# Two squared-ReLU MLPs on one Trainium2 core: weight sums and early low parts move from GpSimd to VectorE, and the squares read PSUM

## The chip, the cores and the metric

The program runs on one core of one Trainium2 chip. The engines are TensorE (PE; its weight loads are PEld), VectorE (DVE), ScalarE (ACT), GpSimd (POOL) and SyncE (SP), which issues most DMAs. Each works through its own list of instructions in order and waits on semaphores for the others. The metric is the device time of the program in microseconds (us): 2716.86 us is the median of 3 runs before the change (2715.68 to 2720.47).

## What is computed

Two layers of a diffusion backbone with 1024 latent tokens, 256 context tokens and 1024 channels. Layer 0 mixes tokens with a Fourier mixer, layer 1 with windowed attention; each is followed by the same MLP, which is what the change touches:

```python
D_MODEL, SEQ, CTX_LEN, DEPTH, D_FF = 1024, 1024, 256, 2, 4096

def _sq_relu_mlp(h, w1, w2):
    return jnp.square(jax.nn.relu(h @ w1)) @ w2

# per layer i, after the mixer
h_lat = h_lat + g2 * _sq_relu_mlp(_modulate(_rms_norm(h_lat, norm2_g[i]), sh2, sc2), mlp_w1[i], mlp_w2[i])
if not last:   # layer 0 alone
    h_ctx = h_ctx + cg2 * _sq_relu_mlp(_modulate(_rms_norm(h_ctx, norm2_g[i]), csh2, csc2), mlp_w1[i], mlp_w2[i])
```

## The kernel before

**Numbers in two parts.** Every fp32 operand of a matmul is split into a rounded high part and a low part (full minus high), and a product is three matmuls: high by high, high by low, low by high (`mm3`, and lines 1293 to 1295). High parts are copies on ScalarE. Low parts are subtractions (`lo_part`, line 58), on VectorE for activations (`l_al`, `l_acl`, `nl`) and on GpSimd for both weights (`l_w1l`, `l_w2l`).

**Pairs.** `mlp` is called once per layer. It goes over the 4096 hidden rows in 16 pairs of 128-row chunks. The latent tokens are two blocks of 512, and layer 0 has the 256 context tokens as a third block. A pair has two products. In the **first product** PE makes `z` for each block and chunk (lines 51 to 53, 24 matmuls each): B11, B12, B22, B21 by block and chunk, and in layer 0 also C0 and C1 for the context. ScalarE applies ReLU from PSUM (`relu`, line 935) into a slot, VectorE squares the slot in place (`square`, line 1123), ScalarE makes the high part (`high`, line 946), VectorE the low part (`low`). The **second product** is done in the Strassen-Winograd manner with 7 block products in place of 8 (`ROWS`: M5, M3, M2, M1, M6, M7, M4). It needs four differences of the hidden blocks, T1 to T4 (`diff`, line 1137, VectorE), and four sums of the second weights' blocks, S1 to S4 (`summed`, line 858, GpSimd). M5 is S1 by T1, M3 is S4 by B22, M2 is A12 by B21, M1 is A11 by B11, M6 is S2 by T2, M7 is S3 by T3, M4 is A22 by T4. Each product is 4 groups of 3 matmuls, one group for each of the four PSUM banks `l_yy_ps`. In layer 0 four context groups (`ctx`, bank `l_yc_ps`) stand among them.

**Reading the groups.** VectorE adds groups 0 to 2 of every product into `ht` with the gate as scale (`acc`, line 1144: PSUM by gate plus `ht`). Group 3 goes through ScalarE (`side_read`, line 953, PSUM into one of two `side` buffers) and GpSimd (`add`, line 880). A PSUM bank is written again only when its last reader is done (`freed`), so M3's group 0 waits for the addition of M5's group 0, and so on.

**What sets the order.** Each engine's list is written out by hand in `mlp`: `hidden` and `outputs` on VectorE and PE, `pair` and `outputs` on ScalarE, `weights` and `outputs` on GpSimd, loads on SP. VectorE's `outputs` puts the difference T4 behind M5's three additions, the low part of B21 (which M2 waits for) behind M3's first, and the low part of T4 behind M2's first. ScalarE's `pair` copies the weights' high parts (`high2`, line 927) between the ReLUs: S1 and A11 behind B11's, A12 and S4 behind B12's. GpSimd's `weights` makes sums and low parts in turn: S1, its low part, S2, A11's low part, S3, A12's low part, S4, S4's low part. Then come the two low parts of the next pair's first weights (`low1`, 1024 wide), then the low parts of the later second weights among the four-bank additions.

**Loads.** SP's list for pair p is `load1(p, 0)`, `load1(p, 1)`, `load2(p)`. A chunk of the first weights is loaded when GpSimd has made the low part of the chunk before it. The second weights of a pair are loaded when all `l_w2l` of the pair before are made. ScalarE's `high1` (line 920) copies a chunk's high part: in pair p, chunk 0 of pair p+1 before B22's ReLU, chunk 1 at the start of `outputs`, ahead of the high part of B21 and the first `side_read`.

## Time and profile before

| | |
|---|---|
| median of 3 runs | 2716.86 us |
| the profiled execution | 2721.47 us, its span 2719.8 us |
| mean granted TensorE clock, share of full speed | 0.955 |
| PE busy | 2406.9 us (88%), 11716 matmuls |
| DVE busy | 1739.2 us (64%) |
| POOL busy | 1205.6 us (44%) |
| ACT busy | 1121.2 us (41%) |
| GpSimd: low parts of second weights (line 58) | 240 of 1372 ns mean |
| GpSimd: sums of second weights (line 858) | 128 of 1375 ns mean |
| GpSimd: low parts of first weights (line 58) | 64 of 2397 ns mean |
| VectorE: squares 512 wide (line 1123) | 128 of 1266 ns mean |

PE is the engine that is busy nearly throughout, so what counts in the two MLPs is where PE stands idle. The share of busy time says little about the others; the timeline does, where it shows which of them ended PE's wait. Layer 0's MLP takes the span from 402.42 to 1298.98 us, layer 1's from 1939.38 us to the end.

### The profile page before, as it was taken

Reading aid. Unit: us, or ns where it says so; the run is one execution under the profiler, and the core shown is the slowest. Engines: PE = TensorE matmul, PEld = TensorE weight load, DVE = VectorE, ACT = ScalarE, POOL = GpSimd, SP = SyncE. Lnnn points to the kernel's source line nnn. Section 1 sums busy time; section 2 is a strip of 40 time slices with the busy share of each in tenths; the row PEclk is TensorE's granted clock in tenths of the full one; section 3 lists DMA queues with packets and bytes.
Section 4 is the critical chain, followed back from the end, with each engine's and each line's share of the span. In section 5 each row is a group of like instructions: output and inputs, shape, how many; then the busy total and the mean of one; then the engine's idle time right before and its main releaser. Section 6 shows DMA issues by size and latency. Waiting matters only on the chain. (4 is left out here: it accounts for less than half of the span.)

```text
span 2719.8 us, 36933 instructions
## 1 busy us (share of the span) xinstructions
PE 2406.9 (88%) x11716; PEld 1941.5 (71%) x11716; DVE 1739.2 (64%) x2705; ACT 1121.2 (41%) x2036; POOL 1205.6 (44%) x927
## 2 busy tenths in 40 slices
PE   4988968999999999999497888879879999898988
PEld 2667847888888788878286666658567777777777
DVE  4557776566656665566676788862556565757565
ACT  4442143333333333333532788860533333333333
POOL 0000034556555555555200455540256666666664
PEclk9998989999999999999799899989889999999999
DMA  6437511010101111010221211112111110111112
GB/s 229 144 109 278 201 66 36 32 39 31 54 31 36 34 49 36 31 39 16 98 72 51 55 28 28 24 46 78 39 39 54 39 54 31 44 49 39 54 39 78
DMA packets 89164, 171.66 MB, mean 63 GB/s; under 512 B 38145, under 2 KB 48897, under 8 KB 82689
## 3 DMA queue, kind: packets, MB, share of 16 engines
q1 hardware_dynamic: 82416, 137.73, 15.1%
q0 software_dynamic: 3456, 25.17, 2.5%
q10 hardware_dynamic: 3216, 7.86, 0.8%
q8 instruction: 35, 0.57, 0.1%
q14 instruction: 41, 0.33, 0.0%
HBM read 158.16 MB, written 12.58 MB: 63 GB/s over the span
## 5 line engine op out<-in xcount | busy, mean ns | idle before, releaser
L1144 DVE SCALAR_TENSOR_TENSOR ht<-l_yy_ps,mod,ht 128x512 f32<-128x512 f32 x672 | 470.0, 745 | 48.5 <-PE l_yy_ps L1295 48.1
L51 PE MATMUL l_z_ps<-nh,l_w1h 128*128 128x512 f32 (+1 forms) x1280 | 475.3, 371 | 10.1 <-DVE nl L58 4.7
L52 PE MATMUL l_z_ps<-nl,l_w1h 128*128 128x512 f32 (+1 forms) x1280 | 473.4, 370 | 0.0
L53 PE MATMUL l_z_ps<-nh,l_w1l 128*128 128x512 f32 (+1 forms) x1280 | 472.8, 369 | 0.0
L1293 PE MATMUL l_yy_ps<-l_ah,l_w2h 128*128 128x512 f32 x896 | 370.4, 413 | 101.3 <-DVE ht L1144 60.6
L58 POOL TENSOR_TENSOR l_w2l<-l_w2f,l_w2h 128x512 fp32r<-128x512 f32 x240 | 328.5, 1372 | 293.7 <-ACT l_w2h L927 288.6
L880 POOL TENSOR_TENSOR ht<-ht,l_side 128x512 f32<-128x512 f32 x224 | 312.2, 1394 | 183.4 <-ACT l_side L953 179.1
L1123 DVE TENSOR_TENSOR l_slot<-l_slot 128x512 f32<-128x512 f32 x128 | 161.9, 1266 | 360.9 <-ACT l_slot L935 360.7
L1294 PE MATMUL l_yy_ps<-l_al,l_w2h 128*128 128x512 f32 x896 | 361.4, 403 | 0.0
L1295 PE MATMUL l_yy_ps<-l_ah,l_w2l 128*128 128x512 f32 x896 | 360.7, 403 | 0.0
L953 ACT ACTIVATE l_side<-l_yy_ps,mod 128x512 f32<-128x512 f32 x224 | 153.4, 685 | 363.8 <-PE l_yy_ps L1295 363.8
L1293 PEld LDWEIGHTS l_yy_ps<-l_ah,l_w2h 128*128 128x128 f32 x896 | 175.8, 196 | 164.2 <-issue 67.7
L51 PEld LDWEIGHTS l_z_ps<-nh,l_w1h 128*128 128x128 f32 x1280 | 243.0, 190 | 54.9 <-DVE nl L58 7.7
L52 PEld LDWEIGHTS l_z_ps<-nl,l_w1h 128*128 128x128 f32 x1280 | 243.1, 190 | 40.4 <-issue 0.5
L53 PEld LDWEIGHTS l_z_ps<-nh,l_w1l 128*128 128x128 f32 x1280 | 242.9, 190 | 40.5
L946 ACT ACTIVATE l_ah<-l_slot 128x512 fp32r<-128x512 f32 x224 | 140.1, 630 | 286.9 <-DVE l_slot L1123 106.4
L58 POOL TENSOR_TENSOR l_w1l<-l_w1f,l_w1h 128x1024 fp32r<-128x1024 f32 x64 | 153.4, 2397 | 236.6 <-ACT l_w1h L920 236.6
L58 DVE TENSOR_TENSOR l_al<-l_slot,l_ah 128x512 fp32r<-128x512 f32 x224 | 174.3, 802 | 52.5 <-ACT l_ah L946 52.5
L1295 PEld LDWEIGHTS l_yy_ps<-l_ah,l_w2l 128*128 128x128 f32 x896 | 175.0, 195 | 39.2
L1294 PEld LDWEIGHTS l_yy_ps<-l_al,l_w2h 128*128 128x128 f32 x896 | 176.9, 197 | 31.2
L927 ACT ACTIVATE l_w2h<-l_w2f 128x512 fp32r<-128x512 f32 x240 | 144.4, 621 | 106.5 <-POOL l_w2f L858 95.6
L858 POOL TENSOR_TENSOR l_w2f<-l_w2f 128x512 f32<-128x512 f32 x128 | 176.0, 1375 | 13.7 <-DMA l_w2f<-w 6.2
(223 smaller groups left out, 4492.9 us busy)
## 6 DMA issues: line engine op xcount, KB each, us to landing
l_w1f<-w SPq DMA_DIRECT2D x64, 512.0 KB, 3.4
l_w2f<-w SPq DMA_DIRECT2D x64, 512.0 KB, 4.2
maw<-ada SPq DMA_DIRECT2D x24, 1024.0 KB, 5.2
aw<-ada POOLq DMA_DIRECT2D x24, 1024.0 KB, 5.1
qb<-queries SPq DMA_DIRECT2D x64, 128.0 KB, 2.7
fw<-fnet_w SPq DMA_DIRECT2D x8, 512.0 KB, 4.5
fx<-x SPq DMA_DIRECT2D x8, 512.0 KB, 5.3
park<-ht SPq DMA_DIRECT2D x1, 4096.0 KB, 12.0
```

Source lines behind the costliest of these rows:

```text
L51: pe.matmul(out, lh, rh, start=first, stop=False)
L52: pe.matmul(out, lh, rl, start=False, stop=False)
L53: return pe.matmul(out, ll, rh, start=False, stop=last)
L58: return eng.tensor_tensor(lo, full, f32(hi), ALU.subtract)
L858: pool.tensor_tensor(w2f[:, PLACE[name]], w2f[:, PLACE[a]], w2f[:, PLACE[b]], op).then_inc(s_sum, 1)
L880: pool.tensor_tensor(h, h, side[(i - 1) % 2][:], ALU.add).then_inc(s_add, 1)
L953: act.activation(side[(i - 1) % 2][:], y_ps[SIDE][:], ACT.Copy, scale=mod[:, layer, G2, m, 0:1]).then_inc(s_ya, 1)
L1123: dve.tensor_tensor(s, s, s, ALU.mult).then_inc(s_sqr, 1)
L1144: dve.scalar_tensor_tensor(out=h, in0=y_ps[m][:], scalar=mod[:, layer, G2, c, 0:1], in1=h, op0=ALU.mult, op1=ALU.add).then_inc(s_acc, 1)
L1293: pe.matmul(y_ps[m][:], wh, a_h, start=first, stop=False, skip_group_check=not first)
L1294: pe.matmul(y_ps[m][:], wh, a_l, start=False, stop=False, skip_group_check=not first)
L1295: pe.matmul(y_ps[m][:], wl, a_h, start=False, stop=True, skip_group_check=not first).then_inc(s_y, 1)
```

## The change

It has six parts, all inside `mlp`:

1. `square` becomes one scalar_tensor_tensor, `max(z, 0) * relu`: its first input is the PSUM bank, its second the slot with ReLU's result. A `z` bank is therefore free for PE when the square is done (`s_sqr`), not when ReLU is (`s_rel`).
2. S1 to S4 and the low parts of S1, A11, A12 and S4 go from GpSimd to VectorE. `weights` stands at the head of VectorE's `hidden`; S4's low part stands behind B11's.
3. GpSimd keeps the low parts of S2, S3, A22 (and A21), of the first weights, and the additions. It has no work in the first product. `low1(p+1, 0)` stands behind the addition of M3, `low1(p+1, 1)` ahead of that of M6.
4. ScalarE copies the high parts of S1, A11 and A12 ahead of B11's ReLU and that of S4 behind B11's high part. `high1(p+1, 1)` moves from the head of `outputs` to the place behind M1's `side_read` (in layer 0 behind A21's high part), ahead of M6's. In layer 1, A22's high part goes ahead of M1's `side_read`.
5. In VectorE's `hidden`, B22's low part stands ahead of the difference T3.
6. One semaphore for the second weights' low parts becomes two (`s_w2e` for the early four, `s_w2l` for the late ones), and `load2` waits for the late ones.

The order of PE's products does not change.

```diff
-    W_ORDER = ["S1", "A11", "A12", "S4", "S2", "S3", "A22"] + (["A21"] if C else [])
+    W_EARLY = ["S1", "A11", "A12", "S4"]
+    W_LATE = ["S2", "S3", "A22"] + (["A21"] if C else [])
+    W_ORDER = W_EARLY + W_LATE
...
                 def load2(p, rows):
-                    sp.wait_ge(s_w2l, p * NW + PRE)
+                    sp.wait_ge(s_w2l, p * NL + PRE)
...
             def _(pool):
                 def outputs(p, more):
+                    add(p, "M5")
+                    low2(p, "S2")
+                    add(p, "M3")
+                    if more:
+                        low1(p + 1, 0)
+                    low2(p, "S3")
+                    add(p, "M2")
+                    if C:
+                        add(p, "M1")
+                    for name in W_LATE[2:]:
+                        low2(p, name)
+                    if not C:
+                        add(p, "M1")
                     if more:
                         low1(p + 1, 1)
-                    low2(p, "S2")
-                    add(p, "M5")
-                    low2(p, "S3")
-                    for prod in ("M3", "M2", "M1"):
-                        add(p, prod)
-                    for name in W_ORDER[6:]:
-                        low2(p, name)
                     for prod in ("M6", "M7", "M4"):
                         add(p, prod)
...
             def _(act):
                 def outputs(p, order, more):
-                    if more:
-                        act.wait_ge(s_z, p * U1 + (PRE + U1))
-                        high1(p + 1, 1)
                     high(p, "B21", order)
                     side_read(p, "M5")
...
                     side_read(p, "M2")
+                    if not C:
+                        high2(p, "A22")
                     side_read(p, "M1")
                     if C:
                         act.wait_ge(s_y, p * NG + (PRE + Y_AT["ctx", 1] + 1))
-                    for name in W_ORDER[6:]:
+                        high2(p, "A22")
+                        high2(p, "A21")
+                    if more:
+                        high1(p + 1, 1)
+
+                def pair(p, more=True):
+                    for name in ("S1", "A11", "A12"):
                         high2(p, name)
                     relu(p, "B11", Z_LOOP)
                     high(p, "B11", Z_LOOP)
-                    for name in ("S1", "A11"):
-                        high2(p, name)
+                    high2(p, "S4")
                     relu(p, "B12", Z_LOOP)
                     high(p, "T1", Z_LOOP)
-                    for name in ("A12", "S4"):
-                        high2(p, name)
...
             def _(dve):
                 def square(p, name, order):
                     s = source(name)
+                    pos = order.index(name)
+                    n = TB[TOK[name][0]][1]
                     dve.wait_ge(s_rel, z_at(p, name, order))
-                    dve.tensor_tensor(s, s, s, ALU.mult).then_inc(s_sqr, 1)
+                    dve.scalar_tensor_tensor(out=s, in0=z_ps[pos % NZ][:, 0:n], scalar=0.0, in1=s, op0=ALU.max, op1=ALU.mult).then_inc(s_sqr, 1)
...
+                def weights(p):
+                    dve.wait_ge(s_w2, p * 32 + 32)
+                    summed(p, "S1", "A21", ALU.add, "A22")
+                    low2(p, "S1")
+                    replaces(p, "S2", "S1")
+                    summed(p, "S2", "S1", ALU.subtract, "A11")
+                    low2(p, "A11")
+                    replaces(p, "S3", "A11")
+                    summed(p, "S3", "A11", ALU.subtract, "A21")
+                    low2(p, "A12")
+                    replaces(p, "S4", "A12")
+                    summed(p, "S4", "A12", ALU.subtract, "S2")
+
                 def hidden(p):
+                    weights(p)
                     square(p, "B11", Z_LOOP)
                     low(p, "B11", HI_LOOP)
+                    low2(p, "S4")
                     square(p, "B12", Z_LOOP)
...
             def _(pe):
-                        pe.wait_ge(s_rel, p * U1 + (PRE + pos - NZ + 1))
+                        pe.wait_ge(s_sqr, p * U1 + (PRE + pos - NZ + 1))
```

How the lists change is best seen in the first pair of layer 1, which stands outside the loop; the loop has the same order but for one `high1`. The names are those of the tiles (`l_w2f` the second weights, `l_w2h` and `l_w2l` their parts, `l_w1l` the first weights' low part, `l_ah` and `l_al` the hidden blocks' parts); "x3" stands for three in a row. Line numbers of the changed program are its own: 871 is `add`, 945 `side_read`, 919 `high2`, 938 `high`, 912 `high1`, 1142 `summed`, 1105 `square`.

GpSimd, from the last sum to the end of the pair, before:

```order
L858 TENSOR_TENSOR l_w2f<-l_w2f 128x512
L58 TENSOR_TENSOR l_w2l<-l_w2f,l_w2h 128x512
L58 TENSOR_TENSOR l_w1l<-l_w1f,l_w1h 128x1024 x2
L58 TENSOR_TENSOR l_w2l<-l_w2f,l_w2h 128x512
L880 TENSOR_TENSOR ht<-ht,l_side 128x512
L58 TENSOR_TENSOR l_w2l<-l_w2f,l_w2h 128x512
L880 TENSOR_TENSOR ht<-ht,l_side 128x512 x3
L58 TENSOR_TENSOR l_w2l<-l_w2f,l_w2h 128x512
L880 TENSOR_TENSOR ht<-ht,l_side 128x512 x3
```

and all of the pair after, on the same engine:

```order
L871 TENSOR_TENSOR ht<-ht,l_side 128x512
L58 TENSOR_TENSOR l_w2l<-l_w2f,l_w2h 128x512
L871 TENSOR_TENSOR ht<-ht,l_side 128x512
L58 TENSOR_TENSOR l_w1l<-l_w1f,l_w1h 128x1024
L58 TENSOR_TENSOR l_w2l<-l_w2f,l_w2h 128x512
L871 TENSOR_TENSOR ht<-ht,l_side 128x512
L58 TENSOR_TENSOR l_w2l<-l_w2f,l_w2h 128x512
L871 TENSOR_TENSOR ht<-ht,l_side 128x512
L58 TENSOR_TENSOR l_w1l<-l_w1f,l_w1h 128x1024
L871 TENSOR_TENSOR ht<-ht,l_side 128x512 x3
```

The sums and four low parts are gone, the addition of M5 comes first, and the two 1024-wide low parts stand apart, among the additions.

ScalarE from the high parts of B22, T2 and T3 to the end of the pair, before:

```order
L946 ACTIVATE l_ah<-l_slot 128x512 x3
L920 ACTIVATE l_w1h<-l_w1f 128x1024 x2
L946 ACTIVATE l_ah<-l_slot 128x512
L953 ACTIVATE l_side<-l_yy_ps,mod 128x512
L927 ACTIVATE l_w2h<-l_w2f 128x512
L946 ACTIVATE l_ah<-l_slot 128x512
L953 ACTIVATE l_side<-l_yy_ps,mod 128x512
L927 ACTIVATE l_w2h<-l_w2f 128x512
L953 ACTIVATE l_side<-l_yy_ps,mod 128x512 x2
L927 ACTIVATE l_w2h<-l_w2f 128x512
L953 ACTIVATE l_side<-l_yy_ps,mod 128x512 x3
```

and after:

```order
L912 ACTIVATE l_w1h<-l_w1f 128x1024
L938 ACTIVATE l_ah<-l_slot 128x512
L945 ACTIVATE l_side<-l_yy_ps,mod 128x512
L919 ACTIVATE l_w2h<-l_w2f 128x512
L938 ACTIVATE l_ah<-l_slot 128x512
L945 ACTIVATE l_side<-l_yy_ps,mod 128x512
L919 ACTIVATE l_w2h<-l_w2f 128x512
L945 ACTIVATE l_side<-l_yy_ps,mod 128x512
L919 ACTIVATE l_w2h<-l_w2f 128x512
L945 ACTIVATE l_side<-l_yy_ps,mod 128x512
L912 ACTIVATE l_w1h<-l_w1f 128x1024
L945 ACTIVATE l_side<-l_yy_ps,mod 128x512 x3
```

The second copy of the first weights now stands behind four side reads and ahead of the last three.

VectorE from the first square to the additions of M5, before:

```order
L1123 TENSOR_TENSOR l_slot<-l_slot 128x512
L58 TENSOR_TENSOR l_al<-l_slot,l_ah 128x512
L1123 TENSOR_TENSOR l_slot<-l_slot 128x512 x2
L1137 TENSOR_TENSOR l_slot<-l_slot 128x512
L58 TENSOR_TENSOR l_al<-l_slot,l_ah 128x512
L1123 TENSOR_TENSOR l_slot<-l_slot 128x512
L1137 TENSOR_TENSOR l_slot<-l_slot 128x512 x2
L58 TENSOR_TENSOR l_al<-l_slot,l_ah 128x512 x3
L1144 SCALAR_TENSOR_TENSOR ht<-l_yy_ps,mod,ht 128x512 x3
```

and after, up to the two squares:

```order
L1142 TENSOR_TENSOR l_w2f<-l_w2f 128x512
L58 TENSOR_TENSOR l_w2l<-l_w2f,l_w2h 128x512
L1142 TENSOR_TENSOR l_w2f<-l_w2f 128x512
L58 TENSOR_TENSOR l_w2l<-l_w2f,l_w2h 128x512
L1142 TENSOR_TENSOR l_w2f<-l_w2f 128x512
L58 TENSOR_TENSOR l_w2l<-l_w2f,l_w2h 128x512
L1142 TENSOR_TENSOR l_w2f<-l_w2f 128x512
L1105 SCALAR_TENSOR_TENSOR l_slot<-l_z_ps,l_slot 128x512
L58 TENSOR_TENSOR l_al<-l_slot,l_ah 128x512
L58 TENSOR_TENSOR l_w2l<-l_w2f,l_w2h 128x512
L1105 SCALAR_TENSOR_TENSOR l_slot<-l_z_ps,l_slot 128x512 x2
```

Seven instructions on the second weights stand ahead of the first square, and an eighth behind the first low part.

## Rows read from the trace of the kernel before

**Rows 1.** Stretches: bounds, length, then PE, PEld, DVE, ACT, POOL busy, clock, DMA.

```profile
470.62:1243.02 772.40, 742.87 (x3867) 631.20 (x3866) 488.36 (x672) 262.75 (x448) 430.94 (x295) 1.00 0.11 37
2010.96:2661.38 650.42, 600.13 (x2521) 487.52 (x2520) 404.06 (x505) 235.75 (x378) 411.29 (x280) 0.96 0.13 45
1939.38:2010.96 71.58, 53.15 (x183) 39.15 (x182) 53.26 (x66) 37.00 (x56) 30.89 (x20) 0.82 0.14 45
```

**Rows 2.** The same columns: first product of layer 0, then of layer 1.

```profile
691.32:718.88 27.56, 27.56 (x146) 23.77 (x145) 12.34 (x14) 8.87 (x16) 13.91 (x10) 1.00 0.05 18
2010.96:2032.71 21.75, 21.75 (x97) 18.02 (x96) 6.30 (x7) 6.78 (x11) 13.04 (x10) 1.00 0.06 23
```

**Rows 3.** Waits, 14 pairs of layer 0: who for whom, us, times, longest.

```profile
PE l_yy_ps L1293 <- DVE l_al L58: 19.1, 14, 1.4
PE l_yy_ps L1293 <- DVE ht L1144: 10.4, 14, 0.7
```

**Rows 4.** Waits, 14 pairs of layer 1.

```profile
PE l_yy_ps L1293 <- DVE ht L1144: 49.2, 14, 3.5
```

**Rows 5.** Timeline of PE, layer 1: start, us, instruction, [idle before it, who ended it].

```profile
2039.10 0.49 PE L1293 MATMUL l_yy_ps<-l_ah,l_w2h 128*128 128x512 f32 x1 [3.50 <-DVE ht L1144]
2043.21 0.50 PE L1293 MATMUL l_yy_ps<-l_ah,l_w2h 128*128 128x512 f32 x1 [1.12 <-DVE l_al L58]
...
2687.03 0.50 PE L1293 MATMUL l_yy_ps<-l_ah,l_w2h 128*128 128x512 f32 x1 [1.01 <-DVE ht L1144]
2690.73 0.47 PE L1293 MATMUL l_yy_ps<-l_ah,l_w2h 128*128 128x512 f32 x1 [0.68 <-DVE l_al L58]
```

**Rows 6.** Timeline of ACT, the same pair of layer 1.

```profile
2022.04 0.60 ACT L935 ACTIVATE l_slot<-l_z_ps 128x512 f32<-128x512 f32 x1 [2.33 <-PE l_z_ps L53]
...
2029.58 0.63 ACT L927 ACTIVATE l_w2h<-l_w2f 128x512 fp32r<-128x512 f32 x1 [2.77 <-POOL l_w2f L858]
...
2031.06 0.58 ACT L935 ACTIVATE l_slot<-l_z_ps 128x512 f32<-128x512 f32 x1
```

**Rows 7.** Timeline of DVE, the same pair.

```profile
2031.67 2.81 DVE L1123 TENSOR_TENSOR l_slot<-l_slot 128x512 f32<-128x512 f32 x1 [4.66 <-ACT l_slot L935]
...
2038.13 2.06 DVE L1144 SCALAR_TENSOR_TENSOR ht<-l_yy_ps,mod,ht 128x512 f32<-128x512 f32 x3
...
2042.05 1.11 DVE L58 TENSOR_TENSOR l_al<-l_slot,l_ah 128x512 fp32r<-128x512 f32 x1
```

**Rows 8.** Timeline of POOL, the same pair.

```profile
2031.54 2.40 POOL L58 TENSOR_TENSOR l_w1l<-l_w1f,l_w1h 128x1024 fp32r<-128x1024 f32 x1
...
2040.86 1.75 POOL L58 TENSOR_TENSOR l_w2l<-l_w2f,l_w2h 128x512 fp32r<-128x512 f32 x1
```

**Rows 9.** Views of single lines: count, shortest/median/longest ns, first and last start.

```profile
L1123 DVE TENSOR_TENSOR l_slot<-l_slot x128: 677/694/2811, 411.3 to 2685.6; 128x512 f32<-128x512 f32 x128
...
L1144 DVE SCALAR_TENSOR_TENSOR ht<-l_yy_ps,mod,ht x672: 731/744/753, 438.2 to 2708.6; 128x512 f32<-128x512 f32 x168
...
L858 POOL TENSOR_TENSOR l_w2f<-l_w2f x128: 1262/1289/1727, 408.2 to 2678.6; 128x512 f32<-128x512 f32 x128
```

**Rows 10.** Timeline of PE, first pair of layer 0, then of layer 1.

```profile
447.08 0.79 PE L1293 MATMUL l_yy_ps<-l_ah,l_w2h 128*128 128x512 f32 x1 [5.71 <-ACT l_side L953]
...
1981.63 0.77 PE L1293 MATMUL l_yy_ps<-l_ah,l_w2h 128*128 128x512 f32 x1 [7.66 <-DVE l_al L58]
1993.15 0.79 PE L1293 MATMUL l_yy_ps<-l_ah,l_w2h 128*128 128x512 f32 x1 [4.42 <-ACT l_side L953]
```

**Rows 11.** Timeline of ACT, first pair of layer 1.

```profile
1976.19 0.63 ACT L927 ACTIVATE l_w2h<-l_w2f 128x512 fp32r<-128x512 f32 x1 [5.76 <-POOL l_w2f L858]
...
1990.95 1.06 ACT L920 ACTIVATE l_w1h<-l_w1f 128x1024 fp32r<-128x1024 f32 x1 [5.92 <-DMA l_w1f<-w]
```

**Rows 12.** DMA issues: instruction, count, KB each, median us to landing.

```profile
l_w1f<-w SPq DMA_DIRECT2D x64, 512.0 KB, 3.4
l_w2f<-w SPq DMA_DIRECT2D x64, 512.0 KB, 4.2
```

More of the change, by code:

```diff
@@ L1027, in _ @@
                 norm(1)
-                for name in ("S1", "A11"):
+                for name in ("S1", "A11", "A12"):
                     high2(0, name)
@@ L1032, in _ @@
                 high(0, "B11", Z_FIRST)
-                for name in ("A12", "S4"):
-                    high2(0, name)
+                high2(0, "S4")
                 if C:
@@ L1049, in _ @@
                 outputs(0, Z_FIRST, True)
+                for prod in ("M6", "M7", "M4"):
+                    side_read(0, prod)
                 with act.Fori(1, PAIRS - 1) as p:
                     pair(p)
-                pair(PAIRS - 1, False)
+                    for prod in ("M6", "M7", "M4"):
+                        side_read(p, prod)
                 last = PAIRS - 1
+                pair(last, False)
                 def out_half(i):
@@ L1165, in hidden @@
                     diff(p, "T2", "B22", "T1", Z_LOOP, HI_LOOP)
+                    low(p, "B22", HI_LOOP)
                     diff(p, "T3", "B22", "B12", Z_LOOP, HI_LOOP)
-                    for name in ("B22", "T2", "T3"):
+                    for name in ("T2", "T3"):
                         low(p, name, HI_LOOP)
@@ L1202, in _ @@
                 norm(1)
+                weights(0)
                 dve.wait_ge(s_nl, 2 * KC)
@@ L1275, in group @@
                             pe.wait_ge(s_al, p * NH + (PRE + horder.index("C1") + 1))
-                            pe.wait_ge(s_w2l, p * NW + (PRE + W_ORDER.index("A12" if m < 2 else "A21") + 1))
+                            for c in range(2):
+                                split2(pe, p, "A%d%d" % (1 + m // 2, c + 1))
                         for j in range(2):
```

67 lines of the change are left out of this document (22 added, 45 removed).

## The prediction, made before the changed kernel ran

> **What bounds the kernel now.** I read the stretches first, then PE's waits, then the timelines of the engines that ended them. The reader should see a pair as a sum: matmuls without a gap, plus what is lost. In the first product nothing is lost: 96 matmuls of 512 columns take 21.75 us in layer 1, 0.2266 us each, and layer 0's 27.56 us hold the same 96 and 5.81 us of context matmuls, PE busy throughout [rows 2]. A pair of layer 1 has 180 matmuls, 40.8 us; the 14 loop pairs take 650.42 / 14 = 46.46 us each, so 5.66 us are lost. A pair of layer 0 would take 27.56 + 84 x 0.2266 + 5.81 = 52.4 us; it takes 772.40 / 14 = 55.17, so 2.77 us are lost [rows 1]. All of it lies in the second product. Over 28 pairs that is 118 us, nearly the ceiling of what any edit to the loops can give.
>
> The waits say where. In layer 1, PE stands 3.50 us in front of M3 (an addition of M5 is late) and 1.12 us in front of M2 (the low part of B21 is late) [rows 4, 5]. In layer 0 it is 10.4 / 14 = 0.74 and 19.1 / 14 = 1.36 us, the same two places [rows 3]. The rest, 1.04 us and 0.67 us a pair, follows the waits: the first matmul takes 0.49 where others take less [rows 5], and in layer 1 the granted clock is 0.96 of full where layer 0's stays at 1.00 [rows 1], so some matmuls run at 1.2 GHz in place of 2.4. I count 0.35 us for each wait that stays and stays short (0.67 / 2).
>
> Why M5's additions are late is seen on the other engines. GpSimd's last sum, S4, comes so late that ScalarE idles 2.77 us for it, up to 2029.58, and B22's ReLU stands behind it in ScalarE's list and starts at 2031.06 [rows 6]. B12's ReLU starts 11.08 us after its first product does, 0.2 us behind the 10.88 us of its two z [rows 2, 6]; B22's could so have started at 2010.96 + 16.3 + 0.2 = 2027.5. It is 3.6 us late, which is the M3 wait. Then the square takes 2.81 us in place of a median 0.69, and ends 0.54 us after a 2.40 us GpSimd low part that had begun just before it [rows 7, 8, 9].
>
> **The change part by part.** *Squares from PSUM.* They take the form of the additions (PSUM and SBUF in, SBUF out): 672 of those took 731 to 753 ns, whatever GpSimd did, while the squares had a median of 694 and went up to 2811 [rows 9]. I take 744, so 0.05 us more on each square that nobody disturbs. One per pair lies on the path (the last before M5's additions): 32 x 0.05 = 1.6 us. The bank is held 0.75 us longer; PE writes it again three or four z later, at least 10 us on, so this is free. The Trainium skill speaks against this part: "VectorE: DVE Perf Modes", section on the TRN2 errata, gives a fixed 120 cycles for a source in PSUM and 58 in SBUF; by its 62 cycles at 0.96 GHz, an estimate of 0.065 us, the part would cost 2.1 us.
>
> *Sums and early low parts on VectorE.* Eight instructions of 0.69 us where GpSimd needed 1.29 [rows 9], and one handover to ScalarE for S1 (0.63 and two short gaps): 5.6 us ahead of B11's square, 0.7 us behind its low part. They start when the last additions are done and the second weights are there. GpSimd's low part of A22 ends about 15 us into the second product by the sum of its new list (six operations of 1.3 us and one of 2.4 from 4.2 us on, with their waits); the load takes 4.2 us each for two issues [rows 12], so it lands about when the product ends. S4 is then ready some 7 us into the first product; before, ScalarE had it 18.6 us in (2029.58). T1 is the first thing that needs these squares, behind B12's ReLU at 11.1 us: 4 us of slack hide the block. Without that cover it would cost what it exceeds, microsecond for microsecond.
>
> *ScalarE.* No copy of a weight stands in front of a late ReLU, so B22's starts at about 16.5 us. M3's wait goes. What is late next is M2's operand. I count from M5's first matmul in layer 1: B21's ReLU ends at 0.8, its square at 1.6, M5's three additions (2.06 [rows 7]) at 3.65, T4 (0.69) at 4.35, M3's first addition at 5.1, and the low part of B21 at 5.8 undisturbed or 6.2 with the 1.11 us that it took beside GpSimd [rows 7, 8]. M2 is due after 24 matmuls, at 5.44. GpSimd's addition of M5 starts at 4.2 in the new list (M5's group 3 ends at 2.9, then the high part of B21 and the side read), so it runs beside this low part: I take 6.2, a wait of 0.7, with bounds of 0.3 and 1.1 (the last pair, where GpSimd had no first weights, shows 0.68; the loop 1.12 [rows 5]). M5's additions precede M3's groups by 0.4 us or more. New loss in layer 1: 0.7 + 0.35 = 1.05, gain 4.6 a pair.
>
> In layer 0 the last block is C1, half as wide, and square, high and low part come before the additions: with half-wide steps bounded by nothing and the full 0.6 to 0.7 each, the additions begin between 0.8 and 2.9; I take 2.0. The same chain ends at 6.5, a wait of 1.05. Loss 1.4, gain 1.4 a pair.
>
> *The first weights' low parts and the load.* `low1` of chunk 0 now ends about 11 us into the second product, chunk 1 lands 3.4 us later [rows 12], at 14.5, and ScalarE copies it until 15.6, ahead of M6's side read, which is due at about 15. PE wants that bank for M7's last group at about 16.6. So it costs nothing in layer 1 with 0.3 us to spare, and in layer 0, whose context groups put M6 3 us later, with more.
>
> *First pairs.* The copy of chunk 1 stood at the head of ScalarE's second product and waited 5.92 us for its DMA in layer 1; the side read of M5 behind it held PE 4.42 us, in layer 0 5.71 [rows 10, 11]. Both go, since that copy now has four side reads before it. PE's 7.66 us before M5 in layer 1 end when T1 is ready, which waited on S4 (ScalarE idle 5.76 us [rows 11]); between nothing and 7.66 comes back, I take 3. For half-rate matmuls (the stretch has a mean clock of 0.82 [rows 1]) I add 2 in each layer: 7.7 + 9.4 = 17, bounds 10 and 24. *Last pair* of layer 1: M3's 1.01 us [rows 5].
>
> **Sum.** 14 x 4.6 + 14 x 1.4 + 17 + 1 = 102 us. The profiled execution took 2721.5, 4.6 us above the median of 2716.9; on the median that gives 2615 us. By the bounds: M2's waits at 0.3 and 0.5 and first pairs at 24 give 2716.9 - 122 = 2595; M2's waits at 1.1 and 1.9 and first pairs at 10 give 2716.9 - 78 = 2639.
>
> **The rivals.** *VectorE falls behind in the second product* (2628 to 2655). If GpSimd's operations catch both low parts in full, B21's and T4's, each loses up to 1.3 us, and the additions of M2 that stand behind T4's low part hold M1 as well. M2's and M1's waits then come to about 2.4 us a pair in both layers and only M3's waits are gained: 14 x (3.50 + 0.74) + 17 + 1 = 77, so 2640. For it: the low part of B21 is caught in the old loop in both layers. Against: later additions have 2.72 us of matmuls for three of 0.70, so 0.6 us per product is made good. The Trainium skill has this as a rule: "SBUF — State Buffer", section "Who interferes with whom", says that a VectorE instruction with two SBUF inputs and a GpSimd instruction that reads SBUF lock each other out for a whole instruction. The trace agrees (2.81 us for 0.69, ending 0.54 us behind GpSimd [rows 7, 8]).
>
> *GpSimd goes on into the next pair.* Its last additions run up to 3 us into the first product and catch VectorE's first sums: 2.6 us more at most, inside the 4 us of slack, no change of time.
>
> *The load stands in front of the side reads* (slower). If the copy of chunk 1 is late, M6's side read is, and PE stops in M7: every us beyond 0.3 (layer 1) or 3 (layer 0) is paid in each pair. To end above 2717 it must cost 102 us, so be late by some 5.4 us in both layers: 14 x (5.1 + 2.4) = 105, 2720 us. ScalarE did wait 5.92 us for this DMA in the first pair [rows 11], but from the end of its previous copy, and with a load time of 3.4 us [rows 12]. A lateness of 1 us costs 10 us.
>
> *The change doesn't do what it says* (M3's wait stays, about 2700): B22's ReLU would have to be late for another reason than S4. 3.6 us late against a wait of 3.50 leaves little.
>
> **How the numbers follow.** The forecast, 2615, has 0.70 (its own range 2595 to 2630). VectorE behind has 0.15, a partial gain between 2650 and 2705 (a late load, or M3's wait staying) has 0.06, less than 2595 (M2's wait gone too) 0.03, nothing at all 0.02, slower 0.04. The range 2595 to 2648 leaves out the last four and the tail of the second: 2 in 10 at most. About 0.2% (5 us) is what a measurement of this kernel can tell from no change: faster 0.94, same 0.02, slower 0.04.
>
> **What would show it.** M3's waits for an addition gone in both layers; one wait of 0.3 to 1.9 us a pair left, in front of M2, ended by the low part of B21; a pair at 41.9 us in layer 1 and 53.8 in layer 0; clock 1.00 in layer 1's loop; squares at 0.74 us without outliers; GpSimd idle in the first product; ScalarE waiting for the first weights' DMA by a few us per pair without PE waiting for the side read. Wrong would be: PE waiting in the first product, or in front of M7 for a side read (the load), or in front of M5 for the low part of T1 (VectorE's new block in the way).

## The result, and the profile after

The changed kernel takes 2609.28 us, the median of four runs from 2607.88 to 2612.35, where the kernel before took 2716.70. The ratio is 0.9604 with a 95% interval from 0.9587 to 0.962: 107 us gained, where 102 were forecast, and the time lies inside the range. The profiled execution after took 2608.24 us with a span of 2606.6; against the profiled one of before that is 113 us, about 6 more than the medians show, since that one had been 4.6 us above its median and this one is 1.0 below.

The stretches after, with the columns of [rows 1]: the 14 loop pairs of layer 0, those of layer 1, the first pair of layer 1, and one first product of layer 1.

```profile
460.40:1208.02 747.62, 741.70 (x3866) 631.24 (x3865) 490.11 (x784) 270.29 (x448) 275.88 (x183) 1.00 0.11 39
1962.39:2549.70 587.31, 579.19 (x2522) 469.74 (x2520) 441.28 (x617) 238.99 (x378) 259.73 (x169) 1.00 0.15 50
1900.36:1962.39 62.03, 50.69 (x182) 37.93 (x181) 54.34 (x74) 37.00 (x56) 18.21 (x12) 0.84 0.15 52
1962.39:1984.15 21.76, 21.76 (x97) 18.02 (x96) 14.02 (x20) 8.79 (x14) 2.83 (x2) 1.00 0.06 23
```

Against [rows 1], layer 0's loop gives back 772.40 - 747.62 = 24.8 us (53.40 us a pair), layer 1's 650.42 - 587.31 = 63.1 (41.95 a pair), and layer 1's first pair 71.58 - 62.03 = 9.6. The first pair of layer 0 goes from 68.20 to 58.45, another 9.8, and the two last pairs give 2.0. These make 109 us; the other 4 of the span lie in code that the change does not touch: from layer 0's last addition to layer 1's first product it took 641.4 us before and 637.8 after, and from 635.8 to 644.6 over all kernels run here. The first product is as long as in [rows 2], 21.76 us, but VectorE works 14.02 us in it where it worked 6.30, and GpSimd 2.83 where it worked 13.04. Layer 1's loop has its clock at 1.00, where [rows 1] had 0.96.

The waits of PE after, first of layer 0's 14 pairs, then of layer 1's (who for whom, us, times, longest). The waits for an addition of [rows 3, 4] are gone. Those for a low part fall from 19.1 to 5.9 us in layer 0; in layer 1, where the view of before has one of 1.1 us in the 14 pairs (the third line), each pair now has one.

```profile
PE l_yy_ps L1306 <- DVE l_al L58: 5.9, 14, 0.4
```

```profile
PE l_yy_ps L1306 <- DVE l_al L58: 8.1, 14, 0.6
```

```profile
PE l_yy_ps L1293 <- DVE l_al L58: 1.1, 1, 1.1
```

The timelines of one second product of layer 1, which starts at 1984.15, answer [rows 5 to 8]. PE, then DVE, POOL and ACT:

```profile
1990.33 0.50 PE L1306 MATMUL l_yy_ps<-l_ah,l_w2h 128*128 128x512 f32 x1 [0.58 <-DVE l_al L58]
```

```profile
1984.98 0.69 DVE L1105 SCALAR_TENSOR_TENSOR l_slot<-l_z_ps,l_slot 128x512 f32<-128x512 f32 x1 [1.36 <-ACT l_slot L927]
1985.59 2.06 DVE L1126 SCALAR_TENSOR_TENSOR ht<-l_yy_ps,mod,ht 128x512 f32<-128x512 f32 x3
...
1988.83 1.45 DVE L58 TENSOR_TENSOR l_al<-l_slot,l_ah 128x512 fp32r<-128x512 f32 x1
```

```profile
1988.44 1.29 POOL L871 TENSOR_TENSOR ht<-ht,l_side 128x512 f32<-128x512 f32 x1 [23.07 <-ACT l_side L945]
```

```profile
1984.35 0.60 ACT L927 ACTIVATE l_slot<-l_z_ps 128x512 f32<-128x512 f32 x1 [1.46 <-PE l_z_ps L53]
...
1999.38 1.06 ACT L912 ACTIVATE l_w1h<-l_w1f 128x1024 fp32r<-128x1024 f32 x1 [2.27 <-DMA l_w1f<-w]
```

The last ReLU now waits for nothing but its own z, the last square takes 0.69 us, M5's additions start 1.44 us into the product, and M3 does not wait. What is left is the low part of B21: 1.45 us beside GpSimd's addition of M5, which had begun 0.39 us before it, and so PE stands 0.58 us in front of M2. ScalarE does wait 2.27 us for the first weights' DMA, and PE not for the side read behind it.

The squares and the additions after, as [rows 9] has them (shortest, median, longest ns):

```profile
L1105 DVE SCALAR_TENSOR_TENSOR l_slot<-l_z_ps,l_slot x128: 681/691/692, 414.3 to 2572.3; 128x512 f32<-128x512 f32 x128
L1126 DVE SCALAR_TENSOR_TENSOR ht<-l_yy_ps,mod,ht x672: 733/743/753, 435.5 to 2595.3; 128x512 f32<-128x512 f32 x168
```

The first pairs after, on PE, against [rows 10]: the waits of 5.71 and 4.42 us for a side read are gone, short waits for the same two places as in the loop have come (0.82 and 1.60, and 0.61), and 5.01 of the 7.66 us before M5 have stayed.

```profile
436.27 0.50 PE L1306 MATMUL l_yy_ps<-l_ah,l_w2h 128*128 128x512 f32 x1 [0.82 <-DVE ht L1126]
440.89 0.47 PE L1306 MATMUL l_yy_ps<-l_ah,l_w2h 128*128 128x512 f32 x1 [1.60 <-DVE l_al L58]
...
1940.06 0.77 PE L1306 MATMUL l_yy_ps<-l_ah,l_w2h 128*128 128x512 f32 x1 [5.01 <-DVE l_al L58]
1948.55 0.47 PE L1306 MATMUL l_yy_ps<-l_ah,l_w2h 128*128 128x512 f32 x1 [0.61 <-DVE l_al L58]
```

### The profile page after: what moved, and what is told of

The parts are those of the page before. It is cut to its first block and busy times, and to the rows that moved or that the text cites. A ratio compares the mean times of both kernels' runs of the same rounds, so it can differ in the third digit from the quotient of the medians.

```text
span 2606.6 us, 37012 instructions
## 1 busy us (share of the span) xinstructions
PE 2374.1 (91%) x11716; PEld 1917.2 (74%) x11716; DVE 1787.0 (69%) x2961; ACT 1131.9 (43%) x2036; POOL 854.7 (33%) x671
## 5 line engine op out<-in xcount | busy, mean ns | idle before, releaser
L871 POOL TENSOR_TENSOR ht<-ht,l_side 128x512 f32<-128x512 f32 x224 | 294.8, 1316 | 940.0 <-ACT l_side L945 933.5
L1306 PE MATMUL l_yy_ps<-l_ah,l_w2h 128*128 128x512 f32 x896 | 358.2, 400 | 23.4 <-DVE l_al L58 22.6
L1307 PE MATMUL l_yy_ps<-l_al,l_w2h 128*128 128x512 f32 x896 | 351.4, 392 | 0.0
L1308 PE MATMUL l_yy_ps<-l_ah,l_w2l 128*128 128x512 f32 x896 | 350.3, 391 | 0.0
L1105 DVE SCALAR_TENSOR_TENSOR l_slot<-l_z_ps,l_slot 128x512 f32<-128x512 f32 x128 | 88.1, 689 | 210.6 <-ACT l_slot L927 210.5
L58 DVE TENSOR_TENSOR l_al<-l_slot,l_ah 128x512 fp32r<-128x512 f32 x224 | 186.5, 834 | 47.6 <-ACT l_ah L938 44.7
L1307 PEld LDWEIGHTS l_yy_ps<-l_al,l_w2h 128*128 128x128 f32 x896 | 169.1, 189 | 27.6
L927 ACT ACTIVATE l_slot<-l_z_ps 128x512 f32<-128x512 f32 x128 | 76.2, 597 | 259.6 <-PE l_z_ps L53 259.6
L58 POOL TENSOR_TENSOR l_w1l<-l_w1f,l_w1h 128x1024 fp32r<-128x1024 f32 x64 | 167.4, 2615 | 28.4 <-ACT l_w1h L912 28.4
L1722 POOL TENSOR_TENSOR sc<-sc,den 128x640 f32<-128x640 f32 x128 | 156.4, 1253 | 18.6 <-DVE den L1816 18.6
```

What stands on the lines that cost most here:

```text
L58: return eng.tensor_tensor(lo, full, f32(hi), ALU.subtract)
L871: pool.tensor_tensor(h, h, side[(i - 1) % 2][:], ALU.add).then_inc(s_add, 1)
L1306: pe.matmul(y_ps[m][:], wh, a_h, start=first, stop=False, skip_group_check=not first)
L1307: pe.matmul(y_ps[m][:], wh, a_l, start=False, stop=False, skip_group_check=not first)
L1308: pe.matmul(y_ps[m][:], wl, a_h, start=False, stop=True, skip_group_check=not first).then_inc(s_y, 1)
L1722: pool.tensor_tensor(sc[:, i, h, 0:KEYS], sc[:, i, h, 0:KEYS], den[:, i, h:h + 1].to_broadcast([P, KEYS]), ALU.mult).then_inc(s_p, 1)
```

## Experiments on what carried the gain

Six kernels do one part alone, undo one, or load one. All times are medians of four runs with the kernel before on the same chip (2716 to 2718 us).

**The squares undone** in the changed kernel: VectorE squares the block in SBUF, and PE's wait for the bank is again one on the ReLU.

```diff
-dve.scalar_tensor_tensor(out=s, in0=z_ps[pos % NZ][:, 0:n], scalar=0.0, in1=s, op0=ALU.max, op1=ALU.mult)
+dve.tensor_tensor(s, s, s, ALU.mult)
```

> The changed kernel, with one part undone: the squares again multiply the slot by itself in SBUF, and PE's next z waits for the ReLU. The theory (order: the gain comes from taking B22's ReLU off the chain of weight sums, and the copy of the first weights off the head of ScalarE's second product) expects no difference: GpSimd is idle throughout the first product in the changed kernel, so a square in SBUF meets nobody. 2609 us, within 4. The rival (squares: reading PSUM keeps the squares out of GpSimd's way, and that is half of the gain) expects the 2.1 us of the old B22 square back in each of 28 pairs: 2609 + 59 = 2668 us.

It took 2609.06 us (ratio 0.9606, 0.959 to 0.9622), as the whole change. Its squares, by the view of their line:

```profile
L1105 DVE TENSOR_TENSOR l_slot<-l_slot x128: 684/692/694, 411.5 to 2567.2; 128x512 f32<-128x512 f32 x128
```

They take the same 0.69 us without one outlier: with nothing of GpSimd left in the first product, there is nothing to escape from.

**The squares alone**, the same edit the other way, put into the kernel before.

> The kernel before, with one part done: squares read PSUM, the rest as it was. The theory expects little: B22's ReLU is still 3.6 us late, and the instruction behind the square, the difference T2, has two SBUF inputs and meets the same 2.40 us GpSimd operation, so it ends about 0.7 us sooner and no more. 28 x 0.7 = 20: 2697 us, PE's wait in front of M3 in layer 1 from 3.5 to about 2.8 us. The rival (squares) expects the whole 2.1 us: 28 x 2.1 = 59, 2658 us, that wait at 1.4 us.

It took 2688.87 us (0.9901, 0.9884 to 0.9918): 28 us gained alone, somewhat more than the 20 expected. PE in one pair of layer 1, and the squares of this kernel:

```profile
2112.73 0.49 PE L1295 MATMUL l_yy_ps<-l_ah,l_w2h 128*128 128x512 f32 x1 [1.55 <-DVE ht L1146]
2117.47 0.50 PE L1295 MATMUL l_yy_ps<-l_ah,l_w2h 128*128 128x512 f32 x1 [1.73 <-DVE l_al L58]
```

```profile
L1125 DVE SCALAR_TENSOR_TENSOR l_slot<-l_z_ps,l_slot x128: 675/691/693, 410.9 to 2652.0; 128x512 f32<-128x512 f32 x128
```

No square is held any more, though GpSimd still works through the first product. M3's wait fell from 3.50 [rows 5] to 1.55, near the 1.4 of the rival, while 1.66 to 1.88 us are lost in front of M2. As the theory had it, the difference T2 now meets the GpSimd operation in the square's place and is held, so this part of the chain gained 0.7 us only; but B22's ReLU also starts 18.9 us into the first product, where it started at 20.1 [rows 2, 6], since S4 came earlier too. In layer 0 M3's wait is gone, and M2 waits 1.37 us as before.

**ScalarE's copies alone** in the new order, in the kernel before.

```diff
+act.wait_ge(s_y, p * NG + PRE)
+for name in ("S1", "A11", "A12"):
+    high2(p, name)
...
-for name in ("S1", "A11"):
-    high2(p, name)
+high2(p, "S4")
...
-for name in ("A12", "S4"):
-    high2(p, name)
```

> The kernel before with ScalarE's copies alone in the new order (S1 and the high parts ahead of the last block's ReLU, S4 behind its high part); squares, sums, low parts and first weights stay where they are. Theory (the order of ScalarE's copies carries most of layer 1): the waits before the second product's M3 go down to about 1 us a pair, 14 x 3.6 + 14 x 0.9 = 63 us, so about 2654. Rival (the order needs the sums on VectorE or the early first weights with it): about 2700, with M3's wait of about 3 us still there.

It took 2671.35 us (0.9826, 0.9808 to 0.9844): 45 us, between the two expectations. PE in one pair of layer 1, and the squares of this kernel:

```profile
2028.56 0.49 PE L1293 MATMUL l_yy_ps<-l_ah,l_w2h 128*128 128x512 f32 x1 [1.06 <-DVE ht L1144]
2032.67 0.50 PE L1293 MATMUL l_yy_ps<-l_ah,l_w2h 128*128 128x512 f32 x1 [1.11 <-DVE l_al L58]
```

```profile
L1123 DVE TENSOR_TENSOR l_slot<-l_slot x128: 679/1174/2506, 411.2 to 2638.7; 128x512 f32<-128x512 f32 x128
```

M3's wait falls to 1.06 us here and 1.11 in the later pairs, as the theory had it, and about 1 us is still lost in front of M2 (0.95 to 1.20 us of standing). So a pair of layer 1 is 2.65 us shorter, 2.4 of them from M3's wait, and not 3.6 us; in layer 0 it is 0.80, not 0.9. That is where the forecast of 2654 failed. What stays of M3's wait: a square that meets GpSimd's long low part still takes up to 2.51 us, and the ReLU and the low parts behind it come late with it.

**First weights back** at their old places, in the changed kernel: GpSimd's low parts for the next pair and ScalarE's second copy for it at the head of the second product (the lines at their new places go).

```diff
 def outputs(p, more):            # GpSimd
+    if more:
+        low1(p + 1, 0)
+        low1(p + 1, 1)
...
 def outputs(p, order, more):     # ScalarE
+    if more:
+        act.wait_ge(s_z, p * U1 + (PRE + U1))
+        high1(p + 1, 1)
```

> The changed kernel, with one part undone: both low parts of the next pair's first weights again at the head of GpSimd's list for the second product, and the copy of chunk 1 again at the head of ScalarE's. Sums stay on VectorE. The theory expects the first pairs' waits back (5.7 and 4.4 us, with some half-rate matmuls 12 in all) and about 0.5 us a pair more in front of M2, because a 2.40 us GpSimd operation runs from about 2 to 4.3 us and pushes T4, the addition of M5 and B21's low part: 2609 + 12 + 13 = 2634 us. If the place of the first weights costs nothing, 2609; if it carries half of the gain, 2660.

It took 2641.37 us (0.9722, 0.9706 to 0.9738), 7 us above the 2634 expected: undone in the finished kernel, the new places are worth 32 us. By the starts of PE's matmuls 15 of them are the first pairs (66.5 and 69.3 us, after 58.5 and 62.0), 13 are layer 0, where M2 waits 1.37 us in place of 0.42, and 4 are layer 1.

**Sums and early low parts on GpSimd** as before, with everything else of the change in place.

```diff
+def weights(p):                  # GpSimd, ahead of outputs(p)
+    pool.wait_ge(s_w2, p * 32 + 32)
+    summed(p, "S1", "A21", ALU.add, "A22")
+    early2(p, "S1")
...
 def pair(p, more=True):          # ScalarE
+    act.wait_ge(s_y, p * NG + PRE)
     for name in ("S1", "A11", "A12"):
...
 def hidden(p):                   # VectorE
-    weights(p)
     square(p, "B11", Z_LOOP)
     low(p, "B11", HI_LOOP)
-    low2(p, "S4")
```

> The changed kernel, with the sums and the four early low parts done by GpSimd again, at the head of its list for a pair, but in the new order: ScalarE still copies S1, A11 and A12 ahead of B11's ReLU, and the first weights stay among the additions. (ScalarE waits for the pair before to be done ahead of its first copy, which it reaches later anyhow.) The theory (order) expects nearly the same time: nine operations of 1.29 us and one copy from about 2.3 us on give S4 at about 13 us of the first product, 2 us after B12's ReLU is due and 3.5 us before B22's; T1 is still in time. Loops unchanged, first pairs 3 to 5 us longer: 2614 us. The rival (engine: it needs VectorE's speed) expects the wait in front of M3 in layer 1 back, 14 x 3.6 = 50, and layer 0's, 14 x 0.9 = 13: 2670 us.

It took 2613.75 us (0.9619, 0.9603 to 0.9635), where 2614 was expected. The pairs of both layers are as long as after the change; what was lost, 4.5 us, lies in the first pairs. So with the rest of the change in place VectorE's speed on these operations, 0.69 us where GpSimd needs 1.29 [rows 9], hardly counts. This kernel squares from PSUM; with squares in SBUF as well it was not run.

**Six more operations on VectorE** per pair of layer 1, behind the last sum: 512 columns each, into a scratch tile that nobody reads.

```diff
+for i in range(EXTRA):
+    dve.wait_ge(s_dum, p * EXTRA + i + PRE)
+    dve.tensor_tensor(scratch[:], w2f[:, PLACE["A22"]], w2f[:, PLACE["S2"]], ALU.subtract).then_inc(s_dum, 1)
```

> The changed kernel with work added: in layer 1, six subtractions of 512 columns into a scratch tile on VectorE behind the sum S4, ahead of B11's square, in every pair (0.72 us each with their waits, 4.3 us). The theory says that the block of weight work is hidden because nothing needs B11's square before B12's ReLU is through: S4 was ready 7 us into the first product and B12's ReLU starts at 11.1, so 4 us more fit: 2609 us, within 4. The rival (VectorE's work in the first product is paid) expects 14 x 4.3 = 60: 2669 us.

It took 2613.51 us (0.9617, 0.9601 to 0.9633). In DVE's timeline the six stand just ahead of the first square:

```profile
2058.41 4.31 DVE L1167 TENSOR_TENSOR l_scratch<-l_w2f 128x512 f32<-128x512 f32 x6
2062.65 0.68 DVE L1109 SCALAR_TENSOR_TENSOR l_slot<-l_z_ps,l_slot 128x512 f32<-128x512 f32 x1
```

Some 60 us more of VectorE's work in 14 pairs left these pairs at 41.9 us; only the first pair, which has no cover, is longer, by 4. The slack of 4 us that the prediction gave the block is there, and there is more: B12's ReLU, which was to be the first to suffer, starts 13.0 us into the first product in place of 11.1, and nothing is lost by it.

The parts therefore do not add up as one would like. Squares alone are worth 28 us, copies alone 45; yet with GpSimd's sums, early low parts and first weights out of the first product, the squares are worth nothing. The squares' edit and the emptying of GpSimd's list remove the same cause, a GpSimd operation beside a square, so where the list is emptied the squares have nothing left to gain.

## Experiments on the wait that was left

**Addition behind the low part** (the add-after-low kernel): GpSimd's addition of M5 also waits until the low part of B21 is done.

```diff
+pool.wait_ge(s_al, p * NH + (PRE + HI_LOOP.index("B21") + 1))
 add(p, "M5")
```

> The changed kernel, with one wait added on GpSimd: its addition of M5 waits for the low part of B21, so that the two no longer run at the same time. The theory (the wait that is left in front of M2 is this collision: the low part took 1.45 us in layer 1 and 1.12 in layer 0 where 0.69 is its undisturbed time) expects M2's wait gone in layer 1 (0.58 us idle, 0.74 with the slower restart) and nearly gone in layer 0 (0.42). But all of GpSimd's list stands 1.1 us later, the load of the next first weights with it, ScalarE's copy of chunk 1 then ends after M7's last group wants its bank, and in layer 1 about 1 us a pair is lost there: 2609 - 14 x 0.4 + 14 x 0.4 = 2609, within 8, with a wait of PE for a side read that was not there. The rival (VectorE is simply late with M5's additions) expects M2's wait to stay as it is, and 2609.

It took 2611.75 us (0.9612, 0.9596 to 0.9628), the same time as the change, and as the theory had it: M2's wait gone, a side read in its place. The rival, which gave the same time, had M2's wait staying. DVE's low part of B21, then PE and ACT in the same product:

```profile
2067.65 0.68 DVE L58 TENSOR_TENSOR l_al<-l_slot,l_ah 128x512 fp32r<-128x512 f32 x1
```

```profile
2072.40 0.50 PE L1307 MATMUL l_yy_ps<-l_ah,l_w2h 128*128 128x512 f32 x1 [0.28 <-DVE ht L1127]
2080.27 0.50 PE L1307 MATMUL l_yy_ps<-l_ah,l_w2h 128*128 128x512 f32 x1 [0.73 <-ACT l_side L946]
```

```profile
2078.58 1.06 ACT L913 ACTIVATE l_w1h<-l_w1f 128x1024 fp32r<-128x1024 f32 x1 [3.01 <-DMA l_w1f<-w]
2079.55 0.67 ACT L946 ACTIVATE l_side<-l_yy_ps,mod 128x512 f32<-128x512 f32 x1
```

The low part falls from 1.45 to 0.68 us and M2's wait is gone, so GpSimd beside it was the cause. In layer 0 a pair gains 0.4 us. In layer 1 PE, now earlier, waits 0.28 us for an addition and then meets the side read behind ScalarE's copy, which waits for the DMA (GpSimd's list, held by the new wait, lets the load begin later too): the late load, one of the prediction's rivals, is the next limit, worth 0.73 us here.

**The copy behind M6's side read** as well.

```diff
 def outputs(p, order, more):
...
+        side_read(p, "M6")
         high1(p + 1, 1)
...
-for prod in ("M6", "M7", "M4"):
+for prod in ("M7", "M4"):
```

> The add-after-low kernel with ScalarE's high part for the next pair put behind M6's side read. Theory (the wait on the side read in layer 1 comes from ScalarE being held by the DMA for that high part): the wait on the side read goes, layer 1's second product takes 19.8 us and layer 0's 25.4, so about 2597. Rival (the side read is late for its own reasons, or the low part of M7 takes the wait over): no gain, 2609 to 2612.

It took 2596.19 us (0.9557, 0.9541 to 0.9573). No pair waits for a side read, layer 1's second product takes 19.75 us and layer 0's 25.44, all as expected.

**Low part first** (the low-part-first kernel): in the changed kernel VectorE takes the low part of B21 right behind M5's additions, and T4 with its low part later, the latter ahead of M2's third addition. ScalarE's copy of T4 goes later with it.

```diff
 for m in range(3):
     acc(p, "M5", m)
-diff(p, "T4", "B21", "T2", zorder, horder)
-acc(p, "M3", 0)
 low(p, "B21", horder)
-acc(p, "M3", 1)
-acc(p, "M3", 2)
+for m in range(3):
+    acc(p, "M3", m)
+diff(p, "T4", "B21", "T2", zorder, horder)
 acc(p, "M2", 0)
-low(p, "T4", horder)
 acc(p, "M2", 1)
+low(p, "T4", horder)
 acc(p, "M2", 2)
...
 high2(p, "S2")                   # ScalarE
-high(p, "T4", order)
 side_read(p, "M3")
 high2(p, "S3")
+high(p, "T4", order)
```

> The changed kernel, reordered on two engines: VectorE makes the low part of B21 directly behind M5's three additions, then M3's three additions, then T4, and T4's low part behind M2's second addition; ScalarE copies T4 behind M3's side read. The low part then ends at 4.3 us of the second product, before GpSimd's addition of M5 begins and before M2 is due at 5.5. The theory expects M2's wait gone in both layers, 14 x (0.74 + 0.58) = 18 us, less what the load of the first weights takes back in layer 1 (M6's side read stands behind a copy that ends 15.5 us in, PE wants the bank at 15.8: up to 0.5 us a pair, 7): 2591 to 2598 us. The rival (VectorE has too much to do there, the wait moves to M3's or M2's additions) expects 2605 to 2612, with PE waiting for an addition instead.

It took 2649.82 us (0.9748, 0.9732 to 0.9764), 40 us slower than the change, against both theories. One product of layer 1 on PE, DVE and POOL:

```profile
2007.64 0.50 PE L1305 MATMUL l_yy_ps<-l_ah,l_w2h 128*128 128x512 f32 x1 [2.24 <-DVE ht L1126]
```

```profile
1999.09 0.69 DVE L58 TENSOR_TENSOR l_al<-l_slot,l_ah 128x512 fp32r<-128x512 f32 x1
...
2004.13 2.80 DVE L58 TENSOR_TENSOR l_al<-l_slot,l_ah 128x512 fp32r<-128x512 f32 x1
2006.85 2.71 DVE L1126 SCALAR_TENSOR_TENSOR ht<-l_yy_ps,mod,ht 128x512 f32<-128x512 f32 x4
```

```profile
2004.01 2.37 POOL L58 TENSOR_TENSOR l_w1l<-l_w1f,l_w1h 128x1024 fp32r<-128x1024 f32 x1
```

M2's wait is gone, as meant. But T4's low part was issued 0.12 us after GpSimd's long low part and ended 0.55 us after that one's end; M2's third addition stands behind it, and PE stands 2.24 us, some 10 us into the product, for the bank which that addition empties (the third group of M1 wants it). Layer 1 pays twice, as two successive pairs show (bounds, length, busy times, then the granted clock):

```profile
2105.94:2151.09 45.15, 42.91 (x182) 34.82 (x180) 32.71 (x45) 17.13 (x27) 18.27 (x12) 0.96 0.14 46
2062.37:2105.94 43.57, 41.33 (x181) 33.63 (x180) 32.60 (x45) 17.14 (x27) 18.26 (x12) 1.00 0.14 48
```

Every second pair is 1.6 us longer at a clock of 0.96: behind that wait six to eight of its matmuls start 0.43 us apart where the others do 0.23, at a granted clock of 0.51 (2140.9 to 2143.3), that is 1.2 GHz in place of 2.4. The same kernel with **ScalarE's copy later** (the edit above) kept the wait:

> As e5_low_first, and ScalarE's copy of chunk 1 moved behind M6's side read, so that no side read of M6 waits for a load. The theory expects no wait of PE left in either loop: 2609 - 18 = 2591 us, a pair of layer 1 at 41.1 to 41.2 us, of layer 0 at 52.8. If the load did no harm in e5, the two are equal; if the copy now holds M7's side read, PE waits in front of M4's last group and the time is above e5's.

It took 2650.28 us (0.9753, 0.9737 to 0.9769). So the place of ScalarE's copy has no part in it.

**T4's low part behind M2's third addition**, on top of that, with GpSimd's list left alone:

```diff
 acc(p, "M2", 1)
-low(p, "T4", horder)
 acc(p, "M2", 2)
+low(p, "T4", horder)
```

> The low-part-first kernel with T4's low part behind M2's third addition, and GpSimd's list left as it was (its long low part for the next pair ahead of that of S3). Theory (whichever VectorE operation on two SBUF tiles is issued while GpSimd's long operation runs waits for its end): M2's additions are no longer held, so the wait of 2.24 us before M2 goes, but T4's low part is held until about 11.4 us into layer 1's second product where it was needed by 10.3, so PE waits about 1.1 us before M1 in each of 14 pairs and the time is 2601 to 2617. Rival (the place of T4's low part alone decides, GpSimd's order does not matter): no wait, 2586 to 2590.

It took 2602.83 us (0.9583, 0.9567 to 0.9599). DVE, POOL and PE in one product of layer 1, which starts at 2016.63:

```profile
2025.92 2.17 DVE L58 TENSOR_TENSOR l_al<-l_slot,l_ah 128x512 fp32r<-128x512 f32 x1
```

```profile
2025.14 2.40 POOL L58 TENSOR_TENSOR l_w1l<-l_w1f,l_w1h 128x1024 fp32r<-128x1024 f32 x1
```

```profile
2028.98 0.49 PE L1306 MATMUL l_yy_ps<-l_ah,l_w2h 128*128 128x512 f32 x1 [1.05 <-DVE ht L1127]
```

The low part, issued 0.78 us into GpSimd's operation, is held again, and PE waits 1.05 us where 1.1 were expected. It does so in front of M6 and not of M1, and it waits for the bank of the addition behind the low part, not for the low part itself.

**GpSimd's low part of S3 ahead of its long one** in addition:

```diff
 add(p, "M3")
+low2(p, "S3")
 if more:
     low1(p + 1, 0)
-low2(p, "S3")
```

> The low-part-first kernel with T4's low part behind M2's third addition, and GpSimd's low part of S3 ahead of its low part for the next pair. Theory (the slower time came from T4's low part issued just behind GpSimd's long operation and from nothing else): the wait of 2.24 us before M2's last matmuls goes to about 0.15, so 2591 to 2597. Rival (another pair of operations meets in the same place): 2609 or more, with a wait of over 0.5 us a pair.

It took 2586.45 us (0.9521, 0.9505 to 0.9537), 23 us better than the change, better than the kernels before it here, and 4.5 us below the range expected. (This kernel ran first; the one above was made after it, to tell its two edits apart: the place of GpSimd's low part of S3 is worth 16 us.) The same low part, and the GpSimd operations around it:

```profile
2022.90 1.06 DVE L58 TENSOR_TENSOR l_al<-l_slot,l_ah 128x512 fp32r<-128x512 f32 x1
```

```profile
2022.11 1.30 POOL L58 TENSOR_TENSOR l_w2l<-l_w2f,l_w2h 128x512 fp32r<-128x512 f32 x1
2023.37 2.86 POOL L58 TENSOR_TENSOR l_w1l<-l_w1f,l_w1h 128x1024 fp32r<-128x1024 f32 x1
```

It meets a short operation in place of a long one, and now GpSimd's long one, issued behind it, takes 2.86 us in place of 2.40. No pair of either loop has a wait left; a pair takes 41.3 us in layer 1 and 52.7 in layer 0, where the prediction counted 40.8 and 52.4 for matmuls without a gap.

## Why the prediction was right

The mechanism held step by step. S4 came 7.1 us into the first product of layer 1 and 6.8 of layer 0 (forecast 7), the last ReLU starts on its z, M3's waits are gone in both layers, one wait a pair is left in front of M2 and is ended by the low part of B21, the clock is 1.00, and ScalarE waits for the load where PE does not. The gain was 107 on the medians against 102. By terms, from the profiled executions:

| term | forecast, us | measured, us |
|---|---|---|
| layer 1, 14 pairs | 64.4 | 63.1 |
| layer 0, 14 pairs | 19.6 | 24.8 |
| first pairs | 17 | 19.3 |
| last pairs | 1 | 2.0 |

**What the 5.66 us of layer 1 were** was read too narrowly. [rows 5] show the first loop pair, and there M2's wait is 1.12 us. In the other 13, M3's wait of 3.5 us is followed by 5 to 13 matmuls that start 0.43 us apart, at 1.2 GHz (granted clock 0.50 from 2085.3 to 2088.0); PE comes to M2 as late as in the first pair (10.5 to 10.7 us in, in three pairs 11.7), and does not stand there. The second loop pair: its stretch (the clock is the 0.96), then two of those matmuls.

```profile
2057.18:2103.26 46.08, 42.58 (x182) 34.75 (x181) 28.79 (x37) 16.82 (x27) 29.25 (x20) 0.96 0.13 46
```

```profile
2086.34 0.63 PE L1295 MATMUL l_yy_ps<-l_ah,l_w2l 128*128 128x512 f32 x1
2086.76 0.63 PE L1293 MATMUL l_yy_ps<-l_ah,l_w2h 128*128 128x512 f32 x1
```

The forecast is not touched by this, since it took the whole 5.66 us, from the lengths, and put in their place what was to stay.

**Layer 0's M2 wait** is the term that was mis-sized: 0.42 us of standing, and a pair of 53.40 us, 1.0 above the gapless 52.4, where 1.05 and 1.4 were forecast. Two small steps made it. The chain was shorter: the additions began 1.87 us into the product and the low part of B21 ended at 6.23, forecast 2.0 and 6.5, since the full 0.6 to 0.7 that I took for C1's half-wide steps was too much (its square and its low part took 0.42 each) and steps overlap by some 0.1. And PE came later than the 5.44 us of 24 matmuls, at 5.7: at M3 two matmuls start 0.32 and 0.33 us apart where others do 0.23, and a few more by 0.23 to 0.24. In layer 1 the forecast wait (0.7) is near the measured one (0.58) by two errors that met: the low part began earlier, 4.68 us in for 5.1, and took 1.45 us for 1.11. The 0.35 us that I put behind each wait were too little in both layers: beyond the standing, a pair loses 0.58 us (53.40 less 52.40 and 0.42 in layer 0; 41.95 less 40.79 and 0.58 in layer 1). So the loss of a pair came out at 1.15 us for 1.05 in layer 1, where the misses partly cancel by luck, and at 1.0 for 1.4 in layer 0, where the shorter wait outweighs.

**The price of a square** was taken from the additions, 744 ns, and is 691. It made no difference of note: 0.05 us on the one square per pair that lies on the path, 1.6 us in all. The Trainium skill ("VectorE: DVE Perf Modes", section on the TRN2 errata) has 62 cycles more for a source in PSUM, by which the estimate was 0.065 us more a square; the runs show none, 0.691 against 0.692 in SBUF.

**First pairs** were guessed at 17 within bounds of 10 and 24: the side reads' waits went, as forecast, and of the 7.66 us in front of M5 2.65 came back, forecast 3. In layer 0, 3.0 of the 9.8 us lie in the first product, for which nothing had been put down; that stretch took from 29.8 to 34.8 us over the kernels run here.

**The rivals.** VectorE did not fall behind in the second product, but the runs show how near it was: the rival's mechanism, T4's low part held by GpSimd with M2's addition behind it, is just what cost 40 us in the low-part-first kernel, where the operations met 0.12 us apart. In the change itself GpSimd caught both low parts, but by less than the rival's 1.3 us each: B21's took 1.45 us and T4's 1.06, and M1 did not wait. The rule of the Trainium skill that was cited for it ("SBUF — State Buffer", section "Who interferes with whom"), that a VectorE instruction with two inputs in SBUF and a GpSimd one that reads SBUF shut each other out, agrees with these traces: 2.80 us for T4's low part in place of 0.69, and 0.68 for B21's in place of 1.45 once the operations were kept apart. The load did not bind, but did by 0.73 us in the add-after-low kernel, where PE came earlier and GpSimd's low part of chunk 0, which the load waits for, ended 12.2 us into the product in place of 11.4: there was little to spare, as forecast (in the change the side read of M6 ended 0.27 to 0.48 us before the group that wants its bank began, and in the first loop pair that group began 0.17 us late). GpSimd's additions in the next pair cost nothing; VectorE's block had its slack.

What stays open is the share of each part in the gain. Since they remove the same cause twice, no single share exists; only what some are worth alone (squares, copies) or undone (squares, sums, first weights) has been measured. The copies were not undone in the finished kernel, no two parts were undone together, and the place of B22's low part was not tried.
